# The last four modulation slots of a two-block transformer kernel, computed on VectorE from transposed pieces

## Chip, cores, metric

One Trainium2 chip, one core. The metric is the device time of the kernel in microseconds, the median of several runs. The kernel before takes 651.52 us (median of 3 runs, 651.27 to 651.76).

## What is computed

Two transformer blocks run one after the other on 256 tokens of width 1024, all in float32. The first block mixes block-sparse and windowed attention. The second one is steered by a condition `c` and ends in a mixture of 16 experts. Only the condition's path matters here:

```python
mod = jnp.einsum('bd,de->be', jax.nn.silu(c), w_mod[l]) + b_mod[l]      # 1024 -> 6 x 1024
mod_c = jnp.einsum('d,de->e', jax.nn.silu(c_ctx), w_mod[l]) + b_mod[l]
sh_a, sc_a, g_a, sh_f, sc_f, g_f = split(mod, 6)
h = modulate(rmsnorm(x, norm_attn[l]), sh_a, sc_a)
hc = modulate(rmsnorm(xc, norm_attn[l]), csh_a, csc_a)
x = x + g_a * mix
h2 = modulate(rmsnorm(x, norm_ffn[l]), sh_f, sc_f)
x = x + g_f * ec_moe(h2, ...)
```

`w_mod` is 1024 x 6144 floats, 24 MB, and each of its numbers is used for one or two products only. Its last third, 1024 x 2048 (8 MB), gives `sc_f` and `g_f`. They are needed late, by the router and the experts, and for `c` alone.

## The kernel before

Five engines run hand-written programs, tied by semaphores. `STREAM` lists the weight slots in the order in which they are loaded: a slot is 128 partitions x 4096 floats, 2 MB. `W..`, `X..`, `WA`, `WB`, `WO0`, `WO1` are projection weights, `C0`, `C1`, `KU0`, `KU1`, `QU` smaller projections, `M0` to `M11` the modulation weights, and `G`, `U`, `D` the experts' weights at the end. `buffer_of` gives each slot its room: the dense part goes through the two halves of `ring` and, from `WA` on, one or two rooms more (`LATE`); the experts use eleven rooms. SyncE (SP) issues the loads strictly in stream order (L745 on): before each it waits until the room's last user is done (`released`), so what stands behind a waiting load waits too.

`DENSE` is the order of the dense products on TensorE (PE), one name for each output bank: `wa00` is branch A, token half 0, column half 0, and so on; `gA`, `gB` are merge gates, `mT` transposes of the merged rows, `cxT` transposes of the context, `ck`, `cc` context projections, `wo` the output projection, `ckv` context keys and values, `hT` transposes of the second block's rows, `kc` transposes of keys, `xa` the second block's input projection. `schedule` (L158) hangs the other work behind these names, and all engines walk through the same list: "split" is the parting of a weight slot into a rounded part (ScalarE, ACT, L827) and its rest (VectorE, DVE, L2144), quarter by quarter, which the products at L1224 read. Two banks (`BANK_OF`) alternate for most products, so that each waits until the one before the last has been copied out.

The modulation is one of these hung-on jobs. `MOD_AFTER` puts slot `M<n>` behind a product; `mod_slot` (L1497) multiplies its two 128-row chunks with the condition as a 32-column stationary operand, four column strips of the array at a time, into bank `MB`:

```python
for k in range(2):
    for j in range(4):
        c = n % 4 * 2 + k
        ins = pe_.matmul(MB[32 * j:32 * j + 32, :], csil[:, c, :], w[:, k, 512 * j:512 * j + 512], ...)
```

After every fourth slot, `KEPT_AFTER` has VectorE add the bias and keep the round's 2048 columns in `modr` (L2164), and `modT<r>` has TensorE turn them, after which VectorE copies them into the columns `mc`. The last round is `M8` (behind `gB10`), `M9` (behind `gB11`), `M10` (behind `clT`), `M11` (behind `ckv11`), kept behind `kc2`, turned as `modT2` behind `xa12`; then VectorE makes `scl[:, 2]` for the router. `g_a` is not turned but sent as a row to DRAM and loaded back spread over all partitions (`gate_row`, L779 and L783).

`load_constants` (L846) has the ACT queue issue sixteen small loads at the start, behind ScalarE's part of `xT11` and ahead of its first split and of its copy of `qa0`.

## Time and profile before

| | us |
|---|---|
| median of 3 runs | 651.52 |
| span of the profiled execution | 649.5 |
| TensorE busy | 586.5 (90%) |
| VectorE busy | 284.1 (44%) |
| ScalarE busy | 219.2 (34%) |
| mean granted TensorE clock | 0.975 |
| DMA, mean | 297 GB/s |

The page gives the profiled execution's span; its own time is not listed apart, so that it is set at the median, 2.0 us above the span. In the 40 slices of the span (16.2 us each) TensorE is busy at 9 tenths or more until about 490 us, with the clock at full; from there to the end DMA moves 420 to 431 GB/s and TensorE waits for experts' weights. The chain that ended last is 69% PE and 19% DMA.

### The profile page before, as it was taken

The numbers are of one execution on the slowest core, as the hardware profiler recorded it, in microseconds if no ns is written. First come the engines' busy times: TensorE is split into PE (matmuls) and PEld (weight loads), VectorE is DVE, ScalarE is ACT, GpSimd is POOL, SyncE is SP. The second block draws the span as 40 slices with busy tenths as digits, with TensorE's granted clock in tenths as the row PEclk, the third lists the DMA queues.
The fourth block names the chain that finished last, engine by engine and source line by source line (L and its number), as shares of the span: only waits on it lengthen the run. The fifth ranks groups of instructions, "written<-read, shape, count | busy, mean of one in ns | idle before, by whom it ended". The sixth has DMA issues, their size and how long they took to land.

```text
span 649.5 us, 8809 instructions
## 1 busy us (share of the span) xinstructions
PE 586.5 (90%) x3506; PEld 375.1 (58%) x3506; DVE 284.1 (44%) x676; ACT 219.2 (34%) x474; POOL 41.9 (6%) x74
## 2 busy tenths in 40 slices
PE   8999999999999999999999899999989865665875
PEld 7988977777866787748755454546353411311232
DVE  3356477675658534468646777235121100100002
ACT  4344443554524522366425865222110100100002
POOL 3000000000000000110001443100000000000000
PEclk9999999999999999999999999999999987879699
DMA  8594865658688686656587521669999999999994
GB/s 355 177 390 142 367 259 200 250 212 343 260 319 328 259 304 246 250 186 244 193 325 269 217 98 39 236 275 338 369 426 429 425 428 426 429 423 431 424 419 180
DMA packets 20765, 193.09 MB, mean 297 GB/s; under 512 B 3698, under 2 KB 5106, under 8 KB 8564
## 3 DMA queue, kind: packets, MB, share of 16 engines
q1 hardware_dynamic: 17124, 189.02, 73.3%
q10 hardware_dynamic: 3312, 1.93, 1.0%
q0 software_dynamic: 288, 1.57, 0.6%
q8 instruction: 28, 0.46, 0.3%
q14 instruction: 13, 0.11, 0.0%
HBM read 190.94 MB, written 1.05 MB: 296 GB/s over the span
## 4 chain that ended last, share of the span: by engine, by line
PE 69%; DMA 19%; DVE 5%; SPq 2%; ACT 2%; issue 1%; POOL 0%; ACTq 0%; POOLq 0%; DVEq 0%
PE bank L1224 27%; DMA ring<-in_stream 18%; PE bank L1201 6%; PE bank L1212 5%; PE bank L1842 5%; PE bank L1507 3%; PE bank L1778 2%; PE bank L1263 2%; SPq L801 2%; PE bank L1706 2%; PE bank L1641 2%; PE bank L1608 2%; PE bank L1764 2%; PE bank L1564 2%; PE bank L1888 1%
## 5 line engine op out<-in xcount | busy, mean ns | idle before, releaser
L1224 PE MATMUL bank<-weight_parts,u_parts 128*128 128x512 f32 (+2 forms) x416 | 125.8, 385 | 1.6 <-DVE weight_parts L2144 1.1
L2144 DVE TENSOR_TENSOR weight_parts<-ring,weight_parts 128x1024 fp32r<-128x1024 f32 (+2 forms) x64 | 73.3, 1180 | 39.6 <-ACT weight_parts L827 37.8
L1224 PEld LDWEIGHTS bank<-weight_parts,u_parts 128*128 128x128 f32 x416 | 75.5, 188 | 19.6 <-issue 3.3
L827 ACT ACTIVATE weight_parts<-ring 128x1024 fp32r<-128x1024 f32 (+2 forms) x64 | 63.8, 1020 | 32.3 <-PE bank L1224 23.5
L1224 PE MATMUL bank<-weight_parts,x_parts 128*128 128x512 f32 (+1 forms) x128 | 48.3, 378 | 0.0
L1224 PE MATMUL bank<-u_parts,weight_parts 128*128 128x256 f32 x192 | 36.6, 287 | 0.9 <-DVE weight_parts L2144 0.6
L1168 POOL TENSOR_TENSOR small<-small 128x1 f32<-128x1 f32 (+1 forms) x14 | 8.3, 596 | 425.7 <-DVE small L2566 200.1
L891 ACT ACTIVATE sp<-sp,small 128x128 f32<-128x128 f32 (+1 forms) x48 | 21.3, 444 | 36.3 <-DVE small L2068 36.3
L1224 PEld LDWEIGHTS bank<-u_parts,weight_parts 128*128 128x128 f32 x192 | 30.4, 191 | 2.3 <-issue 1.2
L1115 ACT ACTIVATE sp<-bank 128x512 f32<-128x512 f32 x4 | 2.4, 597 | 74.8 <-PE bank L1842 74.8
L1224 PE MATMUL bank<-x_parts,weight_parts 128*128 128x256 f32 x96 | 27.1, 283 | 0.0
L1224 PEld LDWEIGHTS bank<-weight_parts,x_parts 128*128 128x128 f32 x128 | 24.0, 188 | 4.5
L1842 PE MATMUL bank<-ring,tz 128*32 128x512 f32 x112 | 16.6, 705 | 10.3 <-DMA ring<-in_stream 10.2
L2538 DVE SCALAR_TENSOR_TENSOR sp<-sp,bank 128x512 f32<-128x512 f32 x4 | 2.7, 687 | 48.2 <-ACT sp L1115 48.2
L1212 PE MATMUL bank<-ring,lat 128*128 128x512 f32 (+2 forms) x56 | 23.2, 556 | 0.4 <-ACT vvc L827 0.4
L2540 DVE TENSOR_TENSOR sp<-sp,bank 128x512 f32<-128x512 f32 x4 | 2.8, 689 | 46.1 <-PE bank L1842 46.1
L1201 PE MATMUL bank<-ident,sp 128*128 128x128 f32 x152 | 21.2, 276 | 1.1 <-DVE sp L2131 0.8
L827 ACT ACTIVATE mo<-bank 128x512 f32<-128x512 f32 (+3 forms) x20 | 10.6, 541 | 33.2 <-PE bank L1224 16.8
L1201 PEld LDWEIGHTS bank<-ident,sp 128*128 128x128 f32 x152 | 17.3, 140 | 6.4 <-issue 3.3
L1764 PEld LDWEIGHTS bank<-modr,rows 128*128 128x128 f32 x128 | 15.0, 191 | 7.9 <-issue 6.9
L2063 DVE CUSTOM_DVE_ANT_0 sp<-bank,tabs 128x128 f32<-128x128 f32 (+1 forms) x48 | 14.3, 354 | 10.0 <-PE bank L1565 9.9
L1224 PEld LDWEIGHTS bank<-x_parts,weight_parts 128*128 128x128 f32 x96 | 18.4, 191 | 0.0
(354 smaller groups left out, 1041.2 us busy)
## 6 DMA issues: line engine op xcount, KB each, us to landing
ring<-in_stream SPq DMA_DIRECT2D x40, 2048.0 KB, 9.0
qk<-in_stream SPq DMA_DIRECT2D x9, 2048.0 KB, 12.3
parts<-in_stream SPq DMA_DIRECT2D x9, 2048.0 KB, 20.1
tabs<-in_stream SPq DMA_DIRECT2D x6, 2048.0 KB, 17.2
mo<-in_stream SPq DMA_DIRECT2D x5, 2048.0 KB, 27.1
vvc<-in_stream SPq DMA_DIRECT2D x5, 2048.0 KB, 30.2
parts<-in_stream SPq DMA_DIRECT2D x6, 1024.0 KB, 34.8
tz<-in_stream SPq DMA_DIRECT2D x4, 1024.0 KB, 24.0
```

The source lines that it names most:

```text
L801: eng.dma_start(slot_columns(name, a, b), stream[n, :, a:b]).then_inc(last_in[h][i], 16)
L827: ins = act.activation(dst, src, ACT.Copy, scale=scale)
L891: ins = act.activation(k, k, ACT.Exp, bias=nm[:, u % 2, 2 * b + q:2 * b + q + 1], accum_out=sums[:, u, 2 * b + q:2 * b + q + 1])
L1201: return pe_.transpose(dst, src, ident[0:n, 0:n])
L1212: ins = pe_.matmul(o, lhs(c), rhs(c), start=(c == 0), stop=(c == chunks - 1))
L1224: ins = pe_.matmul(o, lhs(a, c, i), rhs(b, c, i), start=(c == 0 and n == 0), stop=(c == chunks - 1 and n == 2))
L1263: ins = pe_.matmul(D_(name)[:, S * i:S * i + S], w[:, c, col + P * i:col + P * i + P], u32[:, c, :], start=(c == 0), stop=(c == KC - 1))
L1507: ins = pe_.matmul(MB[32 * j:32 * j + 32, :], csil[:, c, :], w[:, k, 512 * j:512 * j + 512], start=(c == 0), stop=(c == KC - 1), tile_posi ...
L1764: ins = pe_.matmul(o[:, i * P:(i + 1) * P], rn[:, t, c * P:(c + 1) * P], oh[:, t, g * P:(g + 1) * P], start=(t == 0), stop=(t == TOK - 1))
L1842: ins = pe_.matmul(bank[b][32 * e:32 * e + 32, :], xs[:, c, e * CAP:(e + 1) * CAP], w[e][k], start=(c == 0), stop=(c == KC - 1), tile_posi ...
L2063: ins = dve.tensor_tensor_reduce(spn[:, u % 2, b, P * q:P * q + w], src, table[:, h, P * q:P * q + w], 1.0, -3e38, ALU.add, ALU.max, mx[:, ...
L2144: dve.tensor_tensor(quarter(weight_parts[:, SLOT:], name, q), quarter(slot(name), name, q), quarter(weight_parts, name, q).bitcast(F32), A ...
```

## The change

The last third of the modulation leaves the weight stream: `M8` to `M11`, `KEPT_AFTER["kc2"]` and `modT2` go. In their place the host lays `w_mod`'s last 2048 columns out as sixteen pieces of 128 partitions (output columns) x 1024 floats (input rows), 512 KB each. SP loads them beside the stream into four rooms of their own (`vec_at`), four in rotation; VectorE multiplies each with the condition, spread over all partitions (`csil_row`), and sums along the row into one column of `mc`; behind the eighth and the sixteenth it adds the bias. The spread condition is made by a store to DRAM and a load back. `VEC_AFTER` says behind which product VectorE takes which piece, `VEC_LOADS` behind which slot SP asks for it.

```diff
-           "WA", "M6", "W10", "M7", "W11", "M8", "WB", "M9", "C0", "WO0", "WO1", "C1", "M10", "KU0",
-           "X2", "M11", "X1", "X0", "QU", "KU1", "OUT0", "OUT1"]
+           "WA", "M6", "W10", "M7", "W11", "WB", "C0", "WO0", "C1", "WO1", "KU0",
+           "X2", "X1", "X0", "QU", "KU1", "OUT0", "OUT1"]
...
-LATE = {"WO0": 1, "WO1": 4, "C1": 0, "M10": 1, "KU0": 0, "X2": 1, "M11": 5, "X1": 0, "X0": 1, "QU": 0, "KU1": 1, "OUT0": 2, "OUT1": 3}
+LATE = {"C0": 1, "WO0": 4, "C1": 0, "WO1": 1, "KU0": 0, "X2": 1, "X1": 0, "X0": 1, "QU": 0, "KU1": 1, "OUT0": 2, "OUT1": 3}
...
-             "gB10": 8, "gB11": 9, "clT": 10, "ckv11": 11}
-KEPT_AFTER = {"za1": 0, "wa11": 1, "kc2": 2}
+KEPT_AFTER = {"za1": 0, "wa11": 1}
+N_VEC = 16
+VEC_AFTER = {"wa10": [0], "ybT1": [1], "cxT11": [2, 3, 4, 5], "wb00": [6, 7], "mT00": [8, 9], "wo00": [10, 11, 12, 13], "cc0": [14, 15]}
+VEC_LOADS = {"W9": [0, 1], "M7": [2, 3], "W11": [4, 5], "WO0": [6, 7, 8, 9], "C1": [10, 11], "WO1": [12, 13, 14, 15]}
...
+        vec_at = [view(vc, 3072, 1024), view(vc, 4096, 1024), view(vv, 0, 1024), view(pt, 0, 1024)]
...
-                     (rope, "rope"), (nat, "norm_attn"), (nff, "norm_ffn"), (nfc, "norm_final"),
+                     (rope, "rope"), (nat, "norm_attn"), (nff, "norm_ffn"), (nfc, "norm_final"), (vec_bias, "vec_bias"),
...
+                    for i in range(2):
+                        eng.dma_start(bias[i], A["mod_bias"][:, 512 * i:512 * i + 512]).then_inc(bias_in[i], 16)
+                if name == "W5":
+                    eng.wait_ge(cond_ready, 1)
+                    eng.dma_start(cond_row.rearrange("o (p c) -> p (o c)", p=P), csil_col).then_inc(cond_row_out, 16)
+                if name == "M1":
+                    eng.wait_ge(cond_row_out, 16)
+                    eng.dma_start(csil_row, cond_row.to_broadcast([P, D])).then_inc(cond_row_in, 16)
...
-                if name == "C1":
+                if name == "KU0":
                     eng.wait_ge(gate_row_out, 32)
+                    eng.wait_ge(vec_used, 13)
                     eng.dma_start(gG, gate_row.to_broadcast([P, D])).then_inc(gate_row_in, 16)
...
+                for k in VEC_LOADS.get(name, []):
+                    if k == 2:
+                        eng.wait_ge(pvs, len(UNITS))
+                    if k >= 4:
+                        eng.wait_ge(vec_used, k - 3)
+                    eng.dma_start(vec_at[k % 4], A["vecs"][k]).then_inc(vec_in[k % 4], 16)
...
+            def vector_mod(k):
+                if k == 0:
+                    eng.wait_ge(cond_row_in, 16)
+                eng.wait_ge(vec_in[k % 4], 16 * (k // 4 + 1))
+                dve.tensor_tensor_reduce(vec_at[k % 4], vec_at[k % 4], csil_row, 1.0, 0.0, ALU.mult, ALU.add,
+                                         mc[:, 0, 32 + k:33 + k]).then_inc(vec_used, 1)
+                if k % 8 == 7:
+                    a = k - 7
+                    eng.wait_ge(vec_used, k + 1)
+                    own(dve.tensor_tensor(mc[:, 0, 32 + a:40 + a], mc[:, 0, 32 + a:40 + a], vec_bias[:, a:a + 8], ALU.add))
+                    if k == 7:
+                        own(dve.scalar_tensor_tensor(scl[:, 2, :], mc[:, 0, 32:40], 1.0, nff, ALU.add, ALU.mult))
...
-                        if r == 2:
-                            own(dve.scalar_tensor_tensor(scl[:, 2, :], mc[:, 0, 32:40], 1.0, nff, ALU.add, ALU.mult))
```

VectorE also writes the halved condition once more, as `csil_col` (128x8), and three throw-away outputs move from `pt` to `sp`.

The first place is VectorE between the context's transposes (`cxT`, L1976) and branch B's first product (`wb00`, the row that writes `mo`). Before:

```order
L1976 TENSOR_SCALAR tz<-bank,small 128x128 [waits d_ready4]
L1976 TENSOR_SCALAR tz<-bank,small 128x128 x3
L2144 TENSOR_TENSOR weight_parts<-ring,weight_parts 128x1024 [waits split_a] x4
L2313 SCALAR_TENSOR_TENSOR mo<-mo,bank 128x512 [waits d_free0,d_ready0]
L2316 TENSOR_TENSOR tabs<-tabs,mo 128x512 [waits d_free0]
```

Now, with `vec_in` the semaphores of the pieces' loads:

```order
L2176 ISA vvc,small<-vvc,modr 128x1024 [waits vec_in2]
L2176 ISA small 128x1
L2176 ISA pt,small<-pt,modr 128x1024 [waits vec_in3]
L2176 ISA small 128x1
L2176 ISA vvc,small<-vvc,modr 128x1024 [waits vec_in0]
L2176 ISA small 128x1
L2176 ISA vvc,small<-vvc,modr 128x1024 [waits vec_in1]
L2176 ISA small 128x1
L2191 TENSOR_TENSOR weight_parts<-ring,weight_parts 128x1024 [waits split_a] x4
L2363 SCALAR_TENSOR_TENSOR mo<-mo,bank 128x512 [waits d_free0,d_ready0]
L2366 TENSOR_TENSOR tabs<-tabs,mo 128x512 [waits d_free0]
```

Four pieces stand ahead of the split of `WB`.

The second place is SP, from the load of `WO0` on. Before (`qk` is the room of `WO1`, the `ring` loads behind the gate's row are `C1`, `M10` and `KU0`):

```order
L689 DMA qk<-in_stream 128x4096 [waits mod_used]
L779 DMA gate_row<-modr 1x512 [waits mod_kept]
L779 DMA gate_row<-modr 1x512
L689 DMA ring<-in_stream 128x4096 [waits d_ready0]
L783 DMA vvc<-gate_row 128x1024 [waits gate_row_out]
L689 DMA ring<-in_stream 128x4096 [waits split_v]
L689 DMA ring<-in_stream 128x4096 [waits d_ready0]
```

Now (`qk` is the room of `WO0`; the `ring` loads are `C1`, `WO1` and `KU0`):

```order
L708 DMA qk<-in_stream 128x4096 [waits split_v]
L804 DMA gate_row<-modr 1x512 [waits mod_kept]
L804 DMA gate_row<-modr 1x512
L821 DMA vvc<-in_vecs 128x1024 [waits vec_used]
L821 DMA pt<-in_vecs 128x1024 [waits vec_used]
L821 DMA vvc<-in_vecs 128x1024 [waits vec_used] x2
L708 DMA ring<-in_stream 128x4096 [waits split_v]
L821 DMA vvc<-in_vecs 128x1024 [waits vec_used]
L821 DMA pt<-in_vecs 128x1024 [waits vec_used]
L708 DMA ring<-in_stream 128x4096 [waits d_ready0]
L821 DMA vvc<-in_vecs 128x1024 [waits vec_used] x3
L821 DMA pt<-in_vecs 128x1024 [waits vec_used]
L708 DMA ring<-in_stream 128x4096 [waits d_ready0]
L809 DMA vvc<-gate_row 128x1024 [waits vec_used,gate_row_out]
```

Each piece's load waits on SP until VectorE has used the piece four before it, and the slots' loads stand behind these waits.

The third place is TensorE between the transposes `hT01` and `hT11` of the second block's rows. Before:

```order
L1201 MATMUL bank<-ident,rows 128x128 [waits d_free5,normed]
L1201 MATMUL bank<-ident,rows 128x128 x3
L1212 MATMUL bank<-ring,lat 128x512 [waits d_free0]
L1212 MATMUL bank<-ring,lat 128x512
L1507 MATMUL bank<-tabs,small 32x512 [waits slot_in5]
L1507 MATMUL bank<-tabs,small 32x512 x7
L1201 MATMUL bank<-ident,rows 128x128 [waits d_free2,normed]
```

Now:

```order
L1234 MATMUL bank<-ident,rows 128x128 [waits d_free5,normed]
L1234 MATMUL bank<-ident,rows 128x128 x3
L1245 MATMUL bank<-ring,lat 128x512 [waits d_free0]
L1245 MATMUL bank<-ring,lat 128x512
L1234 MATMUL bank<-ident,rows 128x128 [waits d_free2,normed]
```

`M11`'s eight products are gone; the transposes of `hT10` stand directly behind `ckv11`.

## Rows read from the trace of the kernel before

**Rows 1.** Windows: busy of PE, PEld, DVE, ACT, POOL; clock; DMA share; GB/s.
```profile
345.00:400.00 55.00, 52.60 (x288) 27.71 (x285) 41.89 (x120) 36.28 (x101) 20.40 (x37) 1.00 0.46 173
520.00:560.00 40.00, 25.03 (x136) 5.75 (x136) 2.07 (x3) 0.60 (x1) 0.00 (x0) 0.83 1.01 426
```

**Rows 2.** Who waited for whom, SP's queue: total us, times, longest.
```profile
SPq L689 <- PE bank L1608: 20.2, 1, 20.2
```

**Rows 3.** Timeline of PE (start us, us, instruction, idle before): the four slots, modT2, each follower.
```profile
209.77 1.92 PE L1507 MATMUL bank<-ring,small 128*32 128x512 f32 x16
211.63 1.97 PE L1201 MATMUL bank<-ident,vvc 128*128 128x128 f32 x16
...
224.43 1.92 PE L1507 MATMUL bank<-qk,small 128*32 128x512 f32 x16
...
267.70 1.92 PE L1507 MATMUL bank<-ring,small 128*32 128x512 f32 x16
269.56 0.74 PE L1224 MATMUL bank<-weight_parts,u_parts 128*128 128x512 f32 x2
...
288.69 1.93 PE L1507 MATMUL bank<-tabs,small 128*32 128x512 f32 x16
291.93 1.09 PE L1201 MATMUL bank<-ident,rows 128*128 128x128 f32 x8 [1.31 <-DVE rows L1982]
...
305.44 0.60 PE L1201 MATMUL bank<-ident,modr 128*128 128x128 f32 x4
305.79 0.71 PE L1224 MATMUL bank<-weight_parts,u_parts 128*128 128x512 f32 x2
```

**Rows 4.** Timeline of ACT: the copy of wo10 out of its bank.
```profile
267.37 0.60 ACT L827 ACTIVATE rows<-bank 128x512 f32<-128x512 f32 x1 [0.29 <-PE bank L1224]
```

**Rows 5.** Timeline at the start: one ACT load, the copies of qa0 and qa1, PE's kvc.
```profile
15.83 0.45 ACTq L848 DMA_DIRECT2D small<-in_norm_final  x1
...
24.40 1.13 ACT L827 ACTIVATE qk<-bank 128x512 f32<-128x512 f32 x2
25.07 0.36 PE L1224 MATMUL bank<-u_parts,weight_parts 128*128 128x256 f32 x1 [0.17 <-issue]
```

**Rows 6.** Timeline of DVE: the context's two sums of squares, the nearest to a piece.
```profile
200.50 1.22 DVE L2177 CUSTOM_DVE_ANT_0 pt<-vvc 128x1024 f32<-128x1024 f32 x1
201.76 1.23 DVE L2177 CUSTOM_DVE_ANT_0 pt<-vvc 128x1024 f32<-128x1024 f32 x1
```

**Rows 7.** Timeline of DVE: what follows the pieces' places, with the idle time before.
```profile
194.16 0.69 DVE L2306 SCALAR_TENSOR_TENSOR tabs<-mo,bank 128x512 f32<-128x512 f32 x1 [1.42 <-PE bank L1224]
221.61 5.24 DVE L2144 TENSOR_TENSOR weight_parts<-ring,weight_parts 128x1024 fp32r<-128x1024 f32 x4 [6.65 <-ACT weight_parts L827]
235.57 0.69 DVE L2313 SCALAR_TENSOR_TENSOR mo<-mo,bank 128x512 f32<-128x512 f32 x1 [4.78 <-PE bank L1224]
241.14 0.69 DVE L2098 SCALAR_TENSOR_TENSOR ml_parts<-bank,u_parts 128x512 fp32r<-128x512 f32 x1 [3.55 <-ACT u_parts L827]
262.90 0.17 DVE L1957 TENSOR_SCALAR small<-small 128x2 f32<-128x2 f32 x1 [11.36 <-ACT pt L838]
264.68 3.65 DVE L2144 TENSOR_TENSOR weight_parts<-qk,weight_parts 128x1024 fp32r<-128x1024 f32 x3
```

**Rows 8.** DMA issues: KB each, us from issue to landing, alone and behind a slot.
```profile
x_sb<-in_x SPq DMA_DIRECT2D x2, 512.0 KB, 4.2
...
vvc<-gate_row SPq DMA_DIRECT2D x1, 512.0 KB, 9.6
```

**Rows 9.** Timeline of PE: sixteen equal products behind long idle times.
```profile
521.62 3.24 PE L1888 MATMUL bank<-tabs,sp 128*32 128x512 f32 x16 [2.07 <-DMA tabs<-in_stream]
536.29 3.31 PE L1842 MATMUL bank<-parts,tz 128*32 128x512 f32 x16 [2.98 <-DMA parts<-in_stream]
595.15 1.92 PE L1842 MATMUL bank<-ring,tz 128*32 128x512 f32 x16 [2.88 <-DMA ring<-in_stream]
```

**Rows 10.** Windows of one microsecond, columns as in rows 1.
```profile
537.00:538.00 1.00, 1.00 (x9) 0.20 (x4) 0.00 (x0) 0.00 (x0) 0.00 (x0) 0.50 0.92 393
```

More of the change, by code:

```diff
@@ L114 @@
 ROUTER = {"xT10": 2, "xT11": 3, "cxT00": 2, "cxT01": 3, "cxT10": 4, "cxT11": 5, "mT01": 2, "modT1": 3, "mT11": 4,
-          "hT00": 6, "hT01": 5, "modT2": 2, "lq0": 2, "lq1": 3, "lk0": 2, "lk1": 3, "afT": 0, "slT": 1,
+          "hT00": 6, "hT01": 5, "lq0": 2, "lq1": 3, "lk0": 2, "lk1": 3, "afT": 0, "slT": 1,
           "rT00": 2, "rT01": 3, "rT10": 4, "rT11": 5, "rT12": 0, "lgb": 4, "lg0": 2, "ls0": 7, "hT10": 2, "hT11": 3, "kc0": 4, "kc1": 5, "qm0": 4, "qm1": 5, "kx0": 6, "kx1": 7, "lg1": 6, "cuT": 1,
@@ L179, in schedule @@
             out.append(("mod kept", KEPT_AFTER[name]))
+        for k in VEC_AFTER.get(name, []):
+            out.append(("vec", k))
         if name in ROUND_AFTER:
@@ L442, in build @@
         shift_part = tiny(1)
+        vec_bias = tiny(N_VEC)
+        csil_col = tiny(KC)
         affT = view(pt, 1024, 256)
@@ L510, in build @@
         mod_kept = sem("mod_kept")
+        cond_row_out = sem("cond_row_out")
+        cond_row_in = sem("cond_row_in")
+        vec_in = [sem(f"vec_in{i}") for i in range(4)]
+        vec_used = sem("vec_used")
+        cond_row = nc.dram_tensor("cond_row", (1, D), F32, kind="Internal").ap()
         gate_row_out = sem("gate_row_out")
@@ L2176, in _ @@
                     for t in range(TOK):
-                        own(dve.tensor_tensor_reduce(pt[:, 0:D], cn[:, t, :], cn[:, t, :], 1.0, 0.0, ALU.mult,
+                        own(dve.tensor_tensor_reduce(sp[:, 0:D], cn[:, t, :], cn[:, t, :], 1.0, 0.0, ALU.mult,
                                                      ALU.add, ss[:, 2 + t:3 + t]))
@@ L2345, in _ @@
                         leave(ins, name)
-                        eng.wait_ge(split_v, 4 * SPLIT.index("WO1") + 4)
+                        eng.wait_ge(split_v, 4 * SPLIT.index("WO0") + 4)
                         for t in range(TOK):
@@ L2666, in stream_of @@
     wm = chunks(a["w_mod_2"][0])
-    for n in range(12):
+    for n in range(8):
         flat[f"M{n}"] = wm[:, 2 * (n % 4):2 * (n % 4) + 2, 2048 * (n // 4):2048 * (n // 4) + 2048].reshape(P, -1)
@@ L2695, in host_arrays @@
         "norm_ffn": col(a["norm_ffn_2"][0]), "norm_final": col(a["norm_final_2"].reshape(-1)),
-        "mod_bias": mod_bias.reshape(P, -1), "q_norm": col(a["q_norm_2"][0]),
+        "mod_bias": mod_bias.reshape(P, -1), "vec_bias": col(a["b_mod_2"][0, 4096:]),
+        "vecs": a["w_mod_2"][0][:, 4096:].reshape(KC, P, N_VEC, P).transpose(2, 3, 1, 0).reshape(N_VEC, P, D), "q_norm": col(a["q_norm_2"][0]),
         "kv_norm": col(a["kv_norm_2"][0]), "sink": a["sink_2"], "cond": cond, "pe": pe,
```

31 lines of the change are left out of this document (16 added, 15 removed), and 2 rows, old and new, of the table DENSE.

## The prediction

> **What bounds the kernel now.** I read the page's slices first, then the windows, then the timeline of TensorE. Up to about 490 us TensorE is full and its clock is at full speed; after 520 us it is busy 25 of 40 us and DMA moves 426 GB/s [rows 1]. So there are two regimes. In the first, time falls only by what leaves TensorE's own row of work. In the second the expert weights set the pace. What joins them is the point from which the weights can flow: between 345 and 400 us DMA is at 173 GB/s [rows 1], because SP sits up to 20.2 us waiting for TensorE's attention products before it may overwrite a room [rows 2]. Whatever the dense part finishes earlier, the expert loads start earlier, and the end moves by the same amount. I count one to one.
>
> **What leaves TensorE.** A modulation slot is eight float32 products. `M8` starts at 209.77 and the next instruction at 211.63, with no idle time named: 1.86 us [rows 3]. `M9` is the same work in the same place between full neighbours (its row, too, reads 1.92 us): 1.86. `M10` runs from 267.70 to 269.56, again 1.86, but `wo01`, which follows, uses the bank that `wo10` fills, and ScalarE's copy of `wo10` ends only at 267.37 + 0.60 = 267.97 [rows 4]; a waiter starts some 0.05 us behind. So `wo01` can start at 268.02 and the gain is 1.54. `M11` starts at 288.69 and is over by about 290.6; TensorE then sits idle 1.31 us, until VectorE has normalised the rows that `hT10` turns at 291.93 [rows 3]. That chain does not contain `M11`, so its removal gives nothing; the idle time grows from 1.31 to 291.93 - 288.69 = 3.24 us. `modT2` goes from 305.44 to 305.79: 0.35. Sum: 1.86 + 1.86 + 1.54 + 0.35 = 5.61 us. VectorE's third keep, its copies of `modT2` and the making of `scl[:, 2]` leave too, at places where it waits for ScalarE afterwards: nothing.
>
> **What comes to VectorE.** The nearest rows to a piece are the context's two sums of squares, the same instruction on 128x1024: 200.50 and 201.76, so 1.26 us from one to the next, sum read out included [rows 6]. Sixteen make 20.2 us of work, twice what TensorE saves by the clock; it is free only where VectorE idles. The places, before the instruction that must not be late, with its idle time [rows 7]:
> - piece 1 ahead of `wa01` at 194.16: 1.26 of 1.42 (piece 0 lies in an earlier gap, behind `wa10`);
> - pieces 2 to 5 ahead of the split of `WB`, 221.61: 5.04 of 6.65;
> - pieces 6 and 7 and two small ones (some 0.4) ahead of `wb10`, 235.57: 2.9 of 4.78;
> - pieces 8 and 9 ahead of `mT10`, 241.14: 2.52 of 3.55;
> - pieces 10 to 15 ahead of the context's mean, 262.90: 7.6 of 11.36.
>
> All fit, the first by 0.16 us only; a miss there lands on `wa01`'s product with the gate, whose bank TensorE needs four products later. Without `M8` and `M9` TensorE and ScalarE both come earlier by the same amounts, and the gaps, which are waits for them, keep their length. I take 0. If this cover were gone, each piece would cost up to 1.26 us.
>
> **What comes to the queues.** The bytes are the same: four slots of 2 MB, sixteen pieces of 0.5 MB. ScalarE's queue issues one load more (`vec_bias`) in the series in front of its first split. One such issue takes 0.45 us [rows 5]. Behind the series come the split of `W1` and then the copy of `qa0`: it starts at 24.40, takes half of the 1.13 us of the pair and so ends near 25.0, and TensorE's `kvc`, which needs that bank, starts at 25.07 after 0.17 us of idle time [rows 5]. So the load is on the path: 0.46 us lost, less up to 0.17 if the page's "issue" means something else. I take 0.46. The condition's store and load stand on SP behind loads that wait anyway, and their data is used 100 us later: 0.
>
> SP is the riskier queue. Loads 4 to 15 wait there until VectorE has used the piece four before, and slots queue behind them. `C1` stands behind load 9, which waits for piece 5, on the old time scale about 221.61 - 6.65 + 5.04 = 220.0; it may be loaded only when `WB` is split, at 221.61 + 5.24 = 226.85, so it is not held up [rows 7]. `WO1` comes later than before, since its new room is free only when `ck1` is done, shortly before 241.14, and is needed by the split at 264.68 [rows 7], 23 us later; what stood behind a slot landed after 9.6 us [rows 8]. `KU0` stands behind load 15, which waits for piece 11, about 262.90 - 11.36 + 2.52 = 254.1; its own room is free only with `cc1`, whose mean is the row at 262.90 [rows 7]. I take 0 for all three. `X2` can be asked for when `WO1` is split, at about the same time as before.
>
> **The clock.** At the end of the kernel idle times of 2.07 and 2.98 us are followed by sixteen products in 3.24 and 3.31 us, against 1.92 when the clock stays up, as it did once behind 2.88 us [rows 9]; the granted clock behind the second of them is 0.50, so 1.2 GHz for 2.4 [rows 10]. The new idle time of 3.24 us in front of `hT10` is longer than all of these, and before it was 1.31. A fall costs at most 3.31 - 1.92 = 1.4 us by these rows if it lies wholly on TensorE's path, and nothing at the least, if `xa02` waits for VectorE's split of `X2` anyway. That split comes behind `hT11` by way of ScalarE, whose transposes and `hT10`'s (eight in 1.09 us [rows 3]) would take about 1.1 us more at half speed: I take 0.9.
> The Trainium skill (TensorE: Matmul & The Clock Gate, "Part 1: The HAM clock gate") speaks against the change here: it says that an engine which has idled long enough is put on half clock until it has been kept busy again, and that the time at which this is judged runs free of the kernel. By that rule the clock falls in some executions and holds in others, and the sum is 647.3 or 646.4 accordingly; the trace agrees as far as it goes, with 2.88 us that passed and 2.07 that did not.
>
> **Sum.** -5.61 + 0.46 + 0.9 = -4.25 us. The profiled execution, at its span of 649.5, becomes 645.2; with the 2.0 us around it, which I take from the median since its own time isn't listed, 647.3.
>
> **The rivals.**
> 1. The clock holds. For it: the stretch before the gap is full of wide products, unlike the tail's bursts. Against it: two of the three cases in [rows 9]. Then -5.15: 646.4.
> 2. VectorE becomes the wait. The pieces read and write other rooms than the sums of squares did and every gap above has to hold; if the small margins (0.16, 1.0) fail and each piece costs 0.15 us more than its row, or one load is late by a microsecond or two, 1 to 3 us come back: 648 to 650.
> 3. The end is set by something that the dense part doesn't move, and the expert weights flow no earlier. For it: DMA at 426 GB/s after 520 us. Against it: 173 GB/s between 345 and 400 us, with SP waiting for TensorE. Then only noise remains: 651.5.
> 4. Slower, through the last pieces' loads. Load 15 is asked for when piece 11 is done, about 254.1 (old scale), and piece 15 must be through before 262.9, or the mean, then the split of `WO1` at 264.68 and then `wo01` slip. A 512 KB load lands after 4.2 us with little in front of it and 9.6 us behind a slot [rows 8]. At 4.2 it is in time by 3.3 us; at 9.6 piece 15 ends at 265.0, 2.1 late, and since `wo01` needs its first quarter (done at 265.9) only at 268.0, TensorE loses nothing yet. It is slower than before only when the loss passes 5.15 us, that is with a landing time above about 9.6 + 5.2 = 14.8 us; at 17 us 7.4 are lost and the kernel takes 651.5 - 5.15 + 7.4 = 653.8. Against it: nothing large is in the queue there, since `WO1` is asked for before 241.
>
> **How the numbers follow.** A measurement of this kernel can tell about 0.2% (1.3 us) from no change. Chances: forecast 0.42, clock holds 0.34, VectorE 0.12 (a fifth of it above 650.2), weights flow no earlier 0.06, slower 0.06. Forecast and rival 1 hold most; with their unknowns (0.17 us of the ACT load, 0 to 1.4 us of the clock, 0.2 of the waits) they reach from 645.8 to 647.9. To leave out no more than 2 in 10, the range goes up to most of rival 2: 645.8 to 649.6. Faster by over 0.2%: 0.42 + 0.34 + 0.10 = 0.86. Within 0.2%: 0.08. Slower: 0.06.
>
> **What the new profile would show.** Right: PE goes without idle time from `gB10` to the context's transposes and from `gB11` to `wb00`; `wo01` starts 0.05 us behind the copy of `wo10`; in front of `hT10` stands an idle time near 3.2 us released by VectorE's rows, with a clock of 0.50 in a window or two behind it; `kvc` starts near 25.5; VectorE is busy about 303 us; SP's first expert loads come 4 to 5 us earlier. Wrong: idle time of TensorE released by a split of `WB`, `WO0` or `WO1`, or VectorE idle until a load from `vecs`; or the expert loads starting earlier and the end not.

## The result and the profile after

The changed kernel takes 647.57 us (median of 4; 644.74 to 648.44), the kernel before beside it 651.64 (651.27 to 652.29): a ratio of 0.9932, with a 95% interval of 0.9909 to 0.9955. The forecast was 647.3. Two later sessions on other chips gave 646.64 and 645.72 beside 651.06 and 651.05, ratios 0.9933 [0.9907, 0.9959] and 0.9918 [0.9904, 0.9931]. The change gains 4.1 to 5.3 us by these medians; its single executions scatter over 644.5 to 649.6, those of before over 649.9 to 653.0. Two disturbed executions, of 688 us (experiment 1, its profiled one) and 3241 us (experiment 3), are left out of all medians and comparisons.

The profiled execution is that of 648.44 us, span 646.6. TensorE first, as in [rows 3], around the places of `M8` and `M9`, then what stands where `M10` and `M11` were:

```profile
209.90 0.39 PE L1257 MATMUL bank<-weight_parts,x_parts 128*128 128x512 f32 x1
210.13 1.91 PE L1234 MATMUL bank<-ident,vvc 128*128 128x128 f32 x16
...
222.54 0.39 PE L1257 MATMUL bank<-weight_parts,x_parts 128*128 128x512 f32 x1
222.77 0.62 PE L1257 MATMUL bank<-weight_parts,yb_parts 128*128 128x512 f32 x2
...
232.68 3.72 PE L1245 MATMUL bank<-ring,tz 128*128 128x256 f32 x16 [0.40 <-DVE mo L2363]
244.12 0.66 PE L1234 MATMUL bank<-ident,tabs 128*128 128x128 f32 x4 [0.63 <-DVE tabs L2366]
264.39 0.74 PE L1257 MATMUL bank<-weight_parts,u_parts 128*128 128x512 f32 x2 [0.25 <-ACT rows L859]
286.77 1.97 PE L1234 MATMUL bank<-ident,rows 128*128 128x128 f32 x8 [3.18 <-DVE rows L2015]
288.53 0.85 PE L1234 MATMUL bank<-ident,qk 128*96 128x128 f32 x3
```

No idle time where `M8` and `M9` stood; `wo01` waits 0.25 us for ScalarE's copy of `wo10`; in front of `hT10` 3.18 us are idle. The copy itself, against [rows 4], comes 3.63 us earlier:

```profile
263.74 0.60 ACT L859 ACTIVATE rows<-bank 128x512 f32<-128x512 f32 x1 [0.30 <-PE bank L1257]
```

Windows of TensorE from the end of the gap on (columns as in [rows 1]) show the granted clock at 0.50, that is 1.2 GHz, before `hT10` starts at 286.77, and how long it stayed:

```profile
286.00:287.00 1.00, 0.23 (x1) 0.23 (x2) 1.00 (x2) 1.00 (x3) 0.00 (x0) 0.50 0.96 410
...
290.00:291.00 1.00, 1.00 (x8) 0.95 (x6) 0.97 (x3) 0.97 (x3) 0.00 (x0) 0.50 0.90 381
292.00:293.00 1.00, 1.00 (x5) 0.96 (x5) 1.00 (x2) 0.21 (x1) 0.00 (x0) 0.69 0.00 0
293.00:294.00 1.00, 1.00 (x7) 0.99 (x6) 1.00 (x2) 0.00 (x0) 0.00 (x0) 1.00 0.00 0
440.00:441.00 1.00, 1.00 (x2) 0.38 (x2) 0.77 (x6) 0.66 (x3) 0.00 (x0) 0.50 0.99 401
```

The last of these rows is a second fall, in the router's stretch, where TensorE had been busy without a pause. In the profile of before the clock held at both places. VectorE's timeline shows the first two of the four pieces ahead of the split of `WB`, that split, one of the last pieces and the context's mean (compare [rows 7]):

```profile
215.12 1.22 DVE L2176 CUSTOM_DVE_ANT_0 vvc<-vvc,modr 128x1024 f32<-128x1024 f32 x1
...
216.26 1.23 DVE L2176 CUSTOM_DVE_ANT_0 pt<-pt,modr 128x1024 f32<-128x1024 f32 x1
...
220.04 2.53 DVE L2191 TENSOR_TENSOR weight_parts<-ring,weight_parts 128x1024 fp32r<-128x1024 f32 x2 [0.26 <-ACT weight_parts L859]
...
252.71 1.23 DVE L2176 CUSTOM_DVE_ANT_0 vvc<-vvc,modr 128x1024 f32<-128x1024 f32 x1 [0.21 <-DMA vvc<-in_vecs]
...
259.34 0.17 DVE L1990 TENSOR_SCALAR small<-small 128x2 f32<-128x2 f32 x1 [3.97 <-ACT sp L870]
```

A piece takes 1.14 us from one to the next. One of sixteen waits for its load, 0.21 us; 0.26 us are left ahead of the split, and 3.97 us behind the last piece. Next, `kvc`, which [rows 5] had at 25.07, and SP's first load of expert weights, first in before, then in the change (there merged with the second):

```profile
25.52 0.35 PE L1257 MATMUL bank<-u_parts,weight_parts 128*128 128x256 f32 x1 [0.60 <-issue]
```
```profile
344.65 0.33 SPq L689 DMA_DIRECT2D ring<-in_stream  x1
```
```profile
340.14 5.02 SPq L708 DMA_DIRECT2D ring<-in_stream  x2
```

**Where the time went**, as the shift of the same place against before: `kvc` +0.45; the copy of `wo10` -3.63; `wo01` (269.56 before) -5.17; `hT10` (291.93) -5.16; the first expert load -4.51; the span -2.9. So TensorE gave more than forecast up to `hT10`: 5.61 us counted from `kvc` on, against 1.86 + 1.86 + 1.54 = 5.26. Then 0.65 us were lost between `hT10` and the expert loads, and another 1.6 behind them, where the forecast had the shift carried through one to one.

### The profile page after: what moved, and what is told of

Its sections match the earlier page's. It is cut to its first block, busy times and chain, and to the rows that moved or that the text cites. A ratio compares the mean times of both kernels' runs of the same rounds, so it can differ in the third digit from the quotient of the medians.

```text
span 646.6 us, 8720 instructions
## 1 busy us (share of the span) xinstructions
PE 583.8 (90%) x3438; PEld 376.9 (58%) x3438; DVE 302.0 (47%) x708; ACT 219.1 (34%) x474; POOL 42.0 (6%) x74
## 2 busy tenths in 40 slices
DMA packets 22924, 193.35 MB, mean 299 GB/s; under 512 B 4194, under 2 KB 5602, under 8 KB 11236
## 4 chain that ended last, share of the span: by engine, by line
PE 71%; DMA 19%; DVE 3%; SPq 2%; ACT 2%; issue 1%; ACTq 0%; POOL 0%; POOLq 0%; DVEq 0%
PE bank L1257 29%; DMA ring<-in_stream 18%; PE bank L1234 6%; PE bank L1245 6%; PE bank L1875 5%; PE bank L1540 2%; PE bank L1811 2%; PE bank L1296 2%; PE bank L1739 2%; SPq L833 2%; PE bank L1674 2%; PE bank L1641 2%; PE bank L1797 2%; PE bank L1597 2%; PE bank L1921 1%
## 5 line engine op out<-in xcount | busy, mean ns | idle before, releaser
L1875 PE MATMUL bank<-ring,tz 128*32 128x512 f32 x112 | 18.1, 763 | 9.3 <-DMA ring<-in_stream 9.2
```

The lines of the kernel that those rows point to most:

```text
L1875: ins = pe_.matmul(bank[b][32 * e:32 * e + 32, :], xs[:, c, e * CAP:(e + 1) * CAP], w[e][k], start=(c == 0), stop=(c == KC - 1), tile_posi ...
```

## The experiments

All of them are compared at the same places of their profiles: `kvc`, the first product on `ya_parts` (past the stretch that the loads of the ring may pace), `hT10`, and SP's first expert load. Each run has one profile; that of experiment 1 isn't used. The `ya_parts` product is this row of TensorE's timeline, first in before, then in the change:

```profile
185.91 0.73 PE L1224 MATMUL bank<-weight_parts,ya_parts 128*128 128x512 f32 x2 [0.40 <-DVE tabs L2306]
```
```profile
186.36 0.73 PE L1257 MATMUL bank<-weight_parts,ya_parts 128*128 128x512 f32 x2 [0.40 <-DVE tabs L2356]
```

**1. The change again.**

> The changed kernel once more, beside the others. Theory G (the gap in front of hT10 lets the clock fall, in most executions but not in all): median 646.5 to 648.5, the runs more than 2 us apart, and a lower mean clock in the slower ones. Theory N (the falls have nothing to do with the gap; they come and go in the router's and experts' stretches in the kernel before as well): the runs of this kernel and of the one before scatter alike.

Measured: 646.64 us (6 runs), ratio 0.9933 [0.9907, 0.9959]. What scatters is the changed kernel: 644.5 to 649.6, against 650.2 to 653.0 for 17 runs of before. The median and the scatter are those of theory G, but its third sign is missing: the slower executions don't have the lower mean clock (0.975 at 647.47, 0.970 at 644.53, 0.965 at 644.82, 0.966 at 649.62).

**2. The gap filled.** Sixteen transposes that nobody reads stand at `M11`'s old place.

```diff
                 if kind == "dense":
                     dense(n)
+                    if n == "ckv11":
+                        eng.wait_ge(mod_kept, 2)
+                        unread(16, MB)
```

> The changed kernel with sixteen transposes of the identity, read by nobody, on TensorE where M11 stood, behind ckv11. They lie in the idle time before hT10 and so cost nothing themselves. Theory G: idle time before hT10 back to about 1.4 us, no fall there, 0.7 to 1.5 us faster than e1 in the median, about 646.3, and less scatter. Theory N: the same median as e1 within 0.5 us, the same scatter.

Measured: 645.23 us (6 runs, 644.67 to 646.91), ratio 0.9911 [0.9897, 0.9926]. Timeline and one window of TensorE:

```profile
283.89 1.91 PE L1234 MATMUL bank<-ident 128*128 128x128 f32 x16
287.24 1.09 PE L1234 MATMUL bank<-ident,rows 128*128 128x128 f32 x8 [1.44 <-DVE rows L2018]
...
290.00:291.00 1.00, 1.00 (x8) 0.99 (x7) 0.93 (x4) 1.00 (x2) 0.00 (x0) 1.00 1.03 438
```

The idle time is 1.44 us, near the 1.31 with `M11`, the clock holds, and `hT10`'s eight transposes take 1.09 us in place of 1.97. From `hT10` to the first expert load (339.11 here) it is 51.87 us, against 53.37 in the change's profile: beside that execution the useless work is worth 1.5 us, beside the other profiles in which the clock fell 0.3 to 0.4. The median is 1.4 us below experiment 1's, as theory G had it, but it doesn't show what the filling is worth: experiment 4, with the gap left open and the clock down, has the same median in the same session (645.29).

**3. The gap without the change.** In the kernel before, `M11` is multiplied 16 columns wide, which leaves its share of nearly all the sums behind `sc_f` and `g_f` out.

```diff
+                        e = 16 if n in (11,) else 512
-                        ins = pe_.matmul(MB[32 * j:32 * j + 32, :], csil[:, c, :], w[:, k, 512 * j:512 * j + 512],
+                        ins = pe_.matmul(MB[32 * j:32 * j + 32, 0:e], csil[:, c, :], w[:, k, 512 * j:512 * j + e],
```

> The kernel before, in which M11's eight products are 16 columns wide instead of 512: most of round 2's sums (sc_f and g_f) stay incomplete, everything else is kept. Work is taken away and nothing added. Theory G: the idle time before hT10 grows from 1.3 to about 3 us, the clock falls there in most executions, and the kernel gets slower, by 0.7 to 1.5 us in the median (652.3 to 653.1). Theory N: 651.6, no change.

Measured: 651.07 us (11 runs), ratio 1.0003 [0.9992, 1.0014]. TensorE's timeline and window:

```profile
288.74 0.32 PE L1508 MATMUL bank<-tabs,small 128*32 128x16 f32 x16
291.99 1.10 PE L1201 MATMUL bank<-ident,rows 128*128 128x128 f32 x8 [2.93 <-DVE rows L1983]
292.92 2.55 PE L1201 MATMUL bank<-ident,qk 128*96 128x128 f32 x12
...
294.00:296.00 2.00, 2.00 (x10) 1.90 (x9) 1.93 (x6) 1.97 (x5) 0.00 (x0) 0.50 1.01 430
```

`hT10` stays where it was (+0.06), so the removal of `M11` gains nothing, as the forecast had it; with the gap of 2.93 us and nothing else changed the clock falls; and the first expert load comes 0.41 us late (345.06). The price of this fall is 0.35 us from `hT10` on, too little for the median to show. Theory G was right on the fall and wrong on the time (it had 652.3 to 653.1).

**4. The load of `vec_bias` on SP**, at `W9`, with a semaphore of its own.

```diff
-                     (rope, "rope"), (nat, "norm_attn"), (nff, "norm_ffn"), (nfc, "norm_final"), (vec_bias, "vec_bias"),
+                     (rope, "rope"), (nat, "norm_attn"), (nff, "norm_ffn"), (nfc, "norm_final"),
...
                 if name == "W9":
                     kept(eng, "cO1")
+                    eng.dma_start(vec_bias, A["vec_bias"]).then_inc(vec_bias_in, 16)
```

> The changed kernel with the load of vec_bias taken out of ScalarE's first series and issued by SP behind W9. If ScalarE's queue is on the path at the start, as predicted: kvc starts at about 25.07 instead of 25.52, and the median is 0.45 us below e1, as far as the scatter of e1 lets one see. If the series of loads hides it: kvc unchanged at 25.5 and no difference.

Measured: 645.29 us (6 runs), ratio 0.9914 [0.9897, 0.9930]. That is 1.35 us below experiment 1, where the edit was expected to give 0.45; the intervals overlap, and the trace shows no such gain before the expert loads (339.59, against 340.14 and 339.54 in the change's two profiles). `kvc` is back at 25.12, but the stretch behind it isn't:

```profile
71.42 0.85 PE L1362 MATMUL bank<-ring,vvc 128*32 128x128 f32 x22 [0.59 <-DMA ring<-in_stream]
...
83.04 1.92 PE L1542 MATMUL bank<-ring,small 128*32 128x512 f32 x16 [0.37 <-DMA ring<-in_stream]
```

TensorE waits for the ring, 0.96 us in all, which neither before nor the change's first profile showed; the profile with the gap filled has a third such wait (0.45 us at 82.81). This made a new suspect: the change asks for 256 KB of `mod_bias` behind `W3` that were asked for much later before.

**5. The second half of `mod_bias` at `W9`.**

```diff
-                    for i in range(2):
-                        eng.dma_start(bias[i], A["mod_bias"][:, 512 * i:512 * i + 512]).then_inc(bias_in[i], 16)
+                    eng.dma_start(bias[0], A["mod_bias"][:, 0:512]).then_inc(bias_in[0], 16)
...
                 if name == "W9":
                     kept(eng, "cO1")
+                    eng.dma_start(bias[1], A["mod_bias"][:, 512:1024]).then_inc(bias_in[1], 16)
```

> The change with one edit: the second 256 KB of mod_bias, which the change asks for behind W3, is asked for at W9, before the context. Nothing is left out. In the profiles of the change with its gap filled and with the bias load on SP, TensorE waits for a load of the ring at 71.42 (0.59 us) and at 82.8 (0.45 and 0.37 us), and VectorE's split behind 57 us starts at 58.54 to 58.98, against 57.42 and 57.98 in the two profiles of the old order. Theory S (the early half delays the stream): the split starts near 57.7 + 0.45 = 58.1 or earlier, no wait of TensorE for the ring at 71 or 83, and the median is 0.3 to 0.9 us below the change's (646.6 to 647.2, beside 647.5). Theory J (landing times of the loads scatter by themselves): the split starts anywhere between 57.4 and 59.0, and the time is the change's.

Measured: 645.81 us (5 runs), ratio 0.9924 [0.9909, 0.9938], which overlaps that of the change in all its sessions: the time alone doesn't decide. In the trace TensorE doesn't wait for the ring, and from `kvc` (25.96 here) to the `ya_parts` product (186.79) nothing is lost. VectorE's split, in before, in the change and here:

```profile
57.98 2.36 DVE L2144 TENSOR_TENSOR weight_parts<-ring,weight_parts 128x1024 fp32r<-128x1024 f32 x2 [2.88 <-ACT weight_parts L827]
```
```profile
58.54 2.36 DVE L2191 TENSOR_TENSOR weight_parts<-ring,weight_parts 128x1024 fp32r<-128x1024 f32 x2 [2.88 <-ACT weight_parts L859]
```
```profile
57.99 2.36 DVE L2191 TENSOR_TENSOR weight_parts<-ring,weight_parts 128x1024 fp32r<-128x1024 f32 x2 [2.88 <-ACT weight_parts L859]
```

Over all profiles it starts

- at 57.42, 57.98 and 58.14 with the old order (before, experiments 3 and 10),
- at 58.54, 58.63, 58.68, 58.71, 58.97 and 58.98 with the early half (the change and experiments 2, 4, 7, 8 and 11),
- at 57.92, 57.99 and 58.38 with the half moved (experiments 5, 6 and 9).

The second group overlaps neither of the others, though the nearest two are only 0.16 us apart. Its mean is 0.9 us above that of the first and 0.65 above that of the third, in which the half is moved; 256 KB at the 429 GB/s that DMA moves between 30 and 40 us are 0.6 us. The shift arises at VectorE's row L2278 (the change's line number) ahead of the split, which by the code waits for four small copies on ScalarE's queue (`kv2_in`): it starts at 50.50 to 51.20 with the old order, at 51.57 to 52.02 with the early half, at 50.98 to 51.40 with the half moved. Theory S stands for the place; its time was expected at 646.6 to 647.2. This profile holds one thing more: the gap of 3.18 us is there and the clock did not fall (1.00 in the window 290 to 291), so a gap of this size makes the clock fall in most executions, not in all.

**6. The three edits together** (2, 4 and 5).

> The change with three edits at once: sixteen transposes nobody reads in the gap before hT10, the load of vec_bias on SP at W9, and the second half of mod_bias at W9. Nothing is left out. If the three causes (clock fall 0.3 to 1.5 us, kvc late by 0.45, stream late by 0 to 1.0) are separate, the sum of terms with no losses is 651.1 - 5.61 + 0.35 to 0.5 (a wait on VectorE's split in front of xa00 that takes up what modT2 gave): 645.5 to 645.9 by the prediction's own terms, and from the measured 645.2 of the filled gap less 0.45 less some 0.5: 644.3. SP's first expert load (344.65 before, 339.11 with the gap filled) comes at 338.2 to 338.7. If the causes overlap, the time stays at 645.2 and the load at 339.1.

Measured: 645.00 us (5 runs, 643.59 to 645.79), ratio 0.9900 [0.9883, 0.9916]. The first expert load comes at 338.60, as expected of separate causes, though `kvc` came at 25.55 in this profile, as late as with the load of `vec_bias` in the series: one issue on ScalarE's queue took 1.86 us, where the same one (`tri`) takes 1.42 in experiment 4's. The time lies between what the two sums gave (644.3 and 645.5 to 645.9) and isn't clear of the 645.2 of experiment 2.

**7. The pieces tiny, 8. the pieces twice.** In 7 VectorE's products are 8 columns wide, in 8 each is made twice:

```diff
-                dve.tensor_tensor_reduce(vec_at[k % 4], vec_at[k % 4], csil_row, 1.0, 0.0, ALU.mult, ALU.add,
+                dve.tensor_tensor_reduce(vec_at[k % 4][:, 0:8], vec_at[k % 4][:, 0:8], csil_row[:, 0:8], 1.0, 0.0, ALU.mult, ALU.add,
...
+                own(dve.tensor_tensor_reduce(vec_at[k % 4], vec_at[k % 4], csil_row, 1.0, 0.0, ALU.mult, ALU.add,
+                                         mc[:, 0, 32 + k:33 + k]))
```

> The change with VectorE's sixteen products on 8 of 1024 columns; this leaves nearly all of the spread condition's sums out, and with them the values of sh_f and sc_f. All loads and waits stay. VectorE loses 16 x 1.14 us less what a tiny one takes. Theory H (VectorE's work lies in its idle time): median within 0.7 us of the change's, 646.8 to 648.2, and TensorE's remaining waits for VectorE (232.68 with 0.40, 244.12 with 0.63) are as they were. Theory V (part of the 18 us is on the path): 1 to 3 us faster, 644.5 to 646.5, and the first expert load earlier than 339.5.

> The change with each of VectorE's sixteen products made twice, the second on the first one's result; sh_f and sc_f are computed with the squared condition. VectorE gets 16 x 1.2 = 19 us more. By the idle time left in the change's profile in front of wa01 (0.28), the split of WB (0.26), wb10 (2.14), mT10 (1.27) and the context's mean (3.97), the overflow is 0.9, 4.5, 0.3, 1.1 and 3.2 us: theory H (each piece is free only as long as its gap lasts): 4 to 10 us slower than the change, 651.5 to 657.5, with waits of TensorE for a split or a copy behind 215 us. Theory F (idle time of VectorE understates its slack, since TensorE's own backlog absorbs a late split): under 2 us slower, below 649.5.

Measured for 7: 644.88 us (4 runs), ratio 0.9904 [0.9891, 0.9918]. By its median this is theory V's number, and the first expert load (339.45) is 0.05 us below V's bound of 339.5; what lies in between says otherwise:

```profile
233.10 3.72 PE L1245 MATMUL bank<-ring,tz 128*128 128x256 f32 x16 [0.40 <-DVE mo L2363]
244.54 0.66 PE L1234 MATMUL bank<-ident,tabs 128*128 128x128 f32 x4 [0.64 <-DVE tabs L2366]
264.82 0.72 PE L1257 MATMUL bank<-weight_parts,u_parts 128*128 128x512 f32 x2 [0.25 <-ACT rows L859]
287.16 1.13 PE L1234 MATMUL bank<-ident,rows 128*128 128x128 f32 x7 [3.18 <-DVE rows L2015]
```

The waits are those of the change to 0.01 us, and from the `ya_parts` product to `hT10` it is 287.16 - 186.78 = 100.38 us, against 286.77 - 186.36 = 100.41. The sixteen pieces, which all lie in this stretch (190.0 to 255.1 in the change), cost 0.03 us. What the profile gained over the change's first one it gained behind `hT10`, where the clock fell for a shorter time, and not at all at 440. Why all four executions were quick isn't known from one profile.

Measured for 8: 652.10 us (10 runs), ratio 1.0018 [1.0005, 1.0031], slower than before:

```profile
226.23 0.70 PE L1257 MATMUL bank<-weight_parts,yb_parts 128*128 128x512 f32 x2 [3.20 <-DVE weight_parts L2193]
236.81 3.50 PE L1245 MATMUL bank<-ring,tz 128*128 128x256 f32 x15 [0.98 <-DVE mo L2365]
...
269.30 0.66 PE L1234 MATMUL bank<-ident,mo 128*128 128x128 f32 x4 [1.09 <-DVE mo L2389]
270.52 0.70 PE L1257 MATMUL bank<-weight_parts,u_parts 128*128 128x512 f32 x2 [0.56 <-DVE weight_parts L2193]
```

Theory H: the cover ends where VectorE's idle times end. Ahead of the split of `WB`, 4.5 us of overflow became 3.20 us of TensorE's idle time; the first expert load (345.09) is 5.0 and 5.6 us behind those of the change's two profiles. (The values that experiments 7, 8 and 10 spoil are `sc_f` and `g_f`; where their expectations name `sh_f`, that is a slip.)

**9. Four more small loads off ScalarE's queue**, on top of 6 (`norm_final`, `iota`, `tri`, `w_router`).

> The version with three edits, and besides vec_bias four more small loads (norm_final, iota, tri, w_router) taken out of the series on ScalarE's queue and asked for by SP at W9. Nothing is left out. Against the change the queue issues five loads fewer before the first split, 5 x 0.48 = 2.4 us. Theory Q (the series is on the path, as the step on vec_bias says): kvc starts near 25.07 - 4 x 0.48 = 23.1, and the time is up to 1.9 us below that of the three edits (645.0), 643.1. Theory L (the loads of the ring pace the stretch to 83 us): kvc starts early, TensorE then waits for the ring at about 71 and 83 us for what it gained, and the time is within 0.5 us of 645.0.

Measured: 644.43 us (4 runs), ratio 0.9902 [0.9889, 0.9916]. `kvc` starts at 24.51, 0.56 us before [rows 5], then

```profile
24.51 0.47 PE L1262 MATMUL bank<-u_parts,weight_parts 128*128 128x256 f32 x1
...
70.74 1.52 PE L1365 MATMUL bank<-ring,vvc 128*32 128x128 f32 x48 [0.40 <-DMA ring<-in_stream]
...
185.94 0.73 PE L1262 MATMUL bank<-weight_parts,ya_parts 128*128 128x512 f32 x2 [0.40 <-DVE tabs L2366]
```

Theory L: `kvc` has no idle time before it, so the queue paced it only for the first 0.6 us, and those are lost again at 70.74; at 185.94 the kernel is where before was at 185.91. The start at 24.51 is also 1.4 us later than theory Q's 23.1. The 0.57 us under experiment 6 are inside the scatter.

**10. TensorE's saving without VectorE's work.** The edit of experiment 3 on `M8`, `M9` and `M10`, with `M11` whole; the marks for the first and last product of a sum move with it.

> The kernel before with slots M8, M9 and M10 multiplied 16 columns wide in place of 512; this leaves most of their sums out, and with them most of g_f and sh_f; M11 stays whole. All loads and waits stay, VectorE does nothing new. A short slot takes 0.32 us in place of 1.86. Theory T (what leaves TensorE is what the change gains): hT10's transposes start at 291.93 - 3 x 1.54 = 287.3 behind an idle time of about 1.3, the clock stays, and the time is before less 4.6 us, 646.3. Theory E (the end is tied to something else too): less than 3 us below before.

Measured: 646.83 us (5 runs), ratio 0.9937 [0.9924, 0.9949], -4.2 us where 4.6 were expected. The first expert load comes at 340.61, 4.04 early. The idle time in front of `hT10` (287.88, 4.05 early) is 1.33 us and the clock holds; 0.32 us went to one wait for the ring (226.53), and 0.13 us between `kvc` and the `ya_parts` product. Theory T stands.

**11. The change a third time.**

> The change once more, for another profile and its scatter. Nothing is left out. Theory G (a gap of 3.2 us in front of hT10 lets the clock fall, and only the time it stays low scatters): granted clock 0.50 behind 286 us, hT10's eight transposes in 1.9 us, median 646.5 to 648. Theory R (the clock holds in some executions, and in those the time is 644.5): the clock at 1.00 there in this profile if its span is below 643.5. In the stretch 438 to 443 us, where TensorE has no idle time, the clock fell in three of seven profiles; no theory says more of it than that it costs about 1.5 us where it falls.

Measured: 645.72 us (5 runs), ratio 0.9918 [0.9904, 0.9931]; the span of the profile is 644.6. Timeline and windows of TensorE:

```profile
287.35 0.88 PE L1234 MATMUL bank<-ident,rows 128*128 128x128 f32 x6 [3.18 <-DVE rows L2015]
...
288.00:289.00 1.00, 1.00 (x10) 0.98 (x8) 1.00 (x2) 1.00 (x3) 0.00 (x0) 0.78 0.93 397
290.00:291.00 1.00, 1.00 (x6) 0.96 (x5) 0.93 (x4) 0.98 (x2) 0.00 (x0) 0.50 1.13 479
292.00:293.00 1.00, 1.00 (x7) 0.99 (x6) 1.00 (x2) 0.00 (x0) 0.00 (x0) 1.00 0.31 123
```

The clock fell, later than in the first profile (`hT10`'s transposes still ran at the full clock, against G's 1.9 us), and was back by 292. The stretch from `hT10` to the expert load is 52.19 us. The median lies below theory G's 646.5 to 648, and the spread is 1.4 us; theory R's condition, a span below 643.5, didn't occur.

## Why the prediction was right, and where it was right by luck

The time (647.3 against 647.57) and the mechanism (TensorE gives, the end follows by way of the expert loads) were right. The third session's median, 645.72, is 1.6 us below the forecast. The sum was closer than its terms: some gave more than forecast, others that stood at nothing cost something, and that they cancel is luck. All profiles, in us:

| | `kvc` | `ya_parts` | `hT10` | clock behind `hT10` | expert load | clock at 437 to 444 | span |
|---|---|---|---|---|---|---|---|
| before | 25.07 | 185.91 | 291.93 | holds | 344.65 | holds | 649.5 |
| the change | 25.52 | 186.36 | 286.77 | falls | 340.14 | falls | 646.6 |
| 2, gap filled | 25.36 | 186.86 | 287.24 | holds | 339.11 | holds | 643.1 |
| 3, before, short `M11` | 25.10 | 185.94 | 291.99 | falls | 345.06 | holds | 648.6 |
| 4, bias load on SP | 25.12 | 187.05 | 287.43 | falls | 339.59 | holds | 643.7 |
| 5, half later | 25.96 | 186.79 | 287.21 | holds | 339.12 | falls | 644.0 |
| 6, three edits | 25.55 | 186.41 | 286.80 | holds | 338.60 | falls | 643.2 |
| 7, pieces tiny | 25.79 | 186.78 | 287.16 | falls | 339.45 | holds | 643.1 |
| 8, pieces twice | 25.55 | 186.46 | 292.82 | falls | 345.09 | holds | 648.9 |
| 9, small loads moved | 24.51 | 185.94 | 286.32 | holds | 338.23 | falls | 643.3 |
| 10, before, short `M8` to `M10` | 25.06 | 186.03 | 287.88 | holds | 340.61 | falls | 645.3 |
| 11, the change | 25.93 | 186.98 | 287.35 | falls | 339.54 | falls | 644.6 |

**`M8` and `M9`, 1.86 each: too small by 0.2.** The copy of `wo10` comes 3.63 us earlier although the start came 0.45 later, so the two gave 4.08. The step took the distance from the slot's start to the next instruction's. The seams were missing: the transposes start at 210.13, 0.09 us sooner behind a wide product than 209.77 + 0.45, and the pair of products behind `M9` had taken 226.28 to 227.10 and now takes 222.77 to 223.45, 0.14 less. These seams are 0.23 of the missing 0.36; the rest wasn't traced.

**`M10`, 1.54: right to the digit.** `wo01` gained 5.17 - 3.63 = 1.54 and waits 0.25 us for the copy, as told from [rows 4].

**`M11`, nothing: right,** shown by experiment 3, and the idle time is 3.18 us against 3.24.

**`modT2`, 0.35, and VectorE's work around it, nothing: too small by 0.5.** With the clock up, `hT10` to the first expert load takes 51.87, 51.91, 51.80 and 51.91 us (experiments 2, 5, 6, 9), against 52.72 before: 0.85 gained. The wait of 0.50 us for a split at 317.45, in before, is gone in all of them. The forecast cleared VectorE's third keep, its copies and `scl[:, 2]` as work in front of waits for ScalarE. ScalarE's copy into `mo`, VectorE's first instruction on it and the wait, in before, and the first two in experiment 2:

```profile
311.55 0.60 ACT L827 ACTIVATE mo<-bank 128x512 f32<-128x512 f32 x1 [4.44 <-PE bank L1224]
312.58 0.29 DVE L1998 TENSOR_TENSOR sp<-mo,lat 128x128 f32<-128x128 f32 x1 [4.18 <-ACT mo L827]
317.45 0.70 PE L1224 MATMUL bank<-weight_parts,u_parts 128*128 128x512 f32 x2 [0.50 <-DVE weight_parts L2144]
```
```profile
306.40 0.60 ACT L859 ACTIVATE mo<-bank 128x512 f32<-128x512 f32 x1 [4.00 <-PE bank L1257]
307.03 0.29 DVE L2034 TENSOR_TENSOR sp<-mo,lat 128x128 f32<-128x128 f32 x1 [3.70 <-ACT mo L859]
```

VectorE starts 0.43 us behind the end of the copy in before, 0.44 in experiments 3 and 10, and 0.03 in experiments 2, 5 and 6; this brings the split behind it forward. Why it was late at the end of 4.18 us of idle time isn't shown: which of the instructions that went held it wasn't tried apart. Removing only TensorE's slots (experiment 10) leaves the wait (0.51 at 313.38).

**`vec_bias`, 0.46: right in kind, and bounded.** `kvc` is 0.45 late in the change's profile; over the six profiles with the load in the series it is late by 0.29 to 0.89, since two issues of the series take 1.2 to 1.7 us in place of 0.45, each time another length. Without the load it is late by 0.05 (experiment 4) and 0.48 (experiment 6), so that the scatter of the series is as large as the term, and the exact agreement of 0.45 is luck. Experiment 9 shows how far this step reaches: beyond 0.6 us it is the ring that paces.

**The queues, nothing: this step failed.** The bytes in all were nearly the same (193.09 MB before, 193.35 now), the order wasn't. It spoke of the store, the piece loads and the late slots, and passed over the half of `mod_bias` that is asked for behind `W3`. Between `kvc` and the `ya_parts` product the profiles with the early half lose 0, 0.66, 1.09, 0.15, 0.07 and 0.21 us (the change, 2, 4, 7, 8, 11), 0.36 in the mean, nearly all of it from two of them; with the old order experiment 3 loses 0 and experiment 10 loses 0.13, and with the half moved experiments 5 and 6 lose 0 (9 started early and gave its 0.59 back). The piece loads, about which the fourth rival was built, cost VectorE 0.21 us of idle time and TensorE nothing.

**VectorE, nothing: right,** by experiment 7, and the margins were real: doubled, the pieces cost 4.5 to 6.4 us by the medians. The smallest one, 0.16 us ahead of `wa01`, held with 0.28. But one assumption was wrong: that the gaps keep their length. Ahead of the split of `WB` 1.61 us were to be left (6.65 - 5.04), and 0.26 were. VectorE's copies of the context's transposes, first in before, then in the change:

```profile
212.32 2.64 DVE L1976 TENSOR_SCALAR tz<-bank,small 128x128 f32<-128x128 f32 x8
```
```profile
212.56 2.64 DVE L2009 TENSOR_SCALAR tz<-bank,small 128x128 f32<-128x128 f32 x8
```

They follow the split before them and didn't move forward with TensorE, while the split of `WB` did, from 221.61 to 220.04. From the first piece at 215.12 to that split there were 4.92 us, less than the forecast's four pieces at 1.26 (5.04). They fitted because a piece took 1.14: the second error made the first one good.

**The clock, 0.9: right in kind, too large in most executions.** The gap of 2.9 to 3.2 us was followed by a fall of the clock in six of seven profiles, and in the seventh (experiment 5) the first rival's case occurred. The price against 51.87 is 1.50 us in the change's first profile, above the forecast's bound of 1.4, and 0.29, 0.42, 0.40 and 0.32 in the others (4, 7, 8, 11). It depends on when the clock falls and how long it stays, and on the splits that TensorE waits for at the full clock anyway (0.60 us at 292.51 with the gap filled). The Trainium skill (TensorE: Matmul & The Clock Gate, "Part 1: The HAM clock gate") says that the time at which the engine's activity is judged runs free of the kernel. The traces agree: the same 3.18 us were followed by a fall before `hT10` started, by one behind its start, and by none.

**One to one behind the expert loads: only in the mean.** From the first expert load to the end of the span it takes 303.5 to 304.9 us in the six profiles whose clock holds at 437 to 444, and 304.6 to 306.5 in the six where it falls: 304.0 against 305.1 in the mean. It fell in none of the three profiles whose expert loads start near 345 us and in six of nine that start near 340. TensorE has no idle time at 437 to 444. Whether the earlier start brings this about stays open; three profiles are too few to say.

So 6.46 us were given where 5.61 were forecast (5.16 + 0.45 = 5.61 by `hT10`, which only by chance is the same number, and 0.85 behind it), and in the first profile 0.45, 1.5 and 1.6 us were lost again where the sum had 0.46 and 0.9. That execution is the slowest of its four, and its span fell by 2.9 us, not by the 4.25 of the sum. In the median the losses are smaller, and the missed gain and the missed losses cancel. Two small slips of the prediction change nothing: an execution takes 1.8 us more than its span, not 2.0, and its own unknowns reach from 646.0 to 648.0, not from 645.8 to 647.9.

The best version is the change with the three edits, at 645.0 us and a ratio of 0.9900 [0.9883, 0.9916], or with the four small loads moved too (644.4, 0.9902 [0.9889, 0.9916]); the two can't be told apart. Both are below every median measured of the change, but their intervals overlap those of all three of its sessions, so that a gain over the change isn't shown by time. What speaks for the edits is the trace: the first expert load at 338.60 and 338.23, against 340.14 and 339.54.
